# The order in which the sync engine issues the streamed expert tables of a PEER layer

## The reference, cut to what matters

```python
def peer_experts(xn, idx, gates, expert_u, expert_v):
    ...
        u = expert_u[iblk]          # (128 tokens, 128 experts, 1024)
        v = expert_v[iblk]
        act = jax.nn.gelu(jnp.einsum('tkd,td->tk', u, xblk), approximate=False)
        return jnp.einsum('tk,tkd->td', (gblk * act), v)
```

## Time and profile before

| | |
|---|---|
| median of 3 runs | 2571.09 us (2567.44 to 2571.16) |
| profiled execution, its own time | 2571.09 us |
| profiled execution, span from first to last instruction | 2569.4 us |
| TensorE busy | 2479.7 us (97%) |
| VectorE busy | 1968.9 us (77%) |
| GpSimd busy | 1460.1 us (57%) |
| moved by DMA | 857.68 MB, mean 334 GB/s |

### The profile page before, as it was taken

The page is one execution under the profiler, slowest core; times in us unless marked ns, Lnnn a source line. Parts: engine busy times, 40 slices in busy tenths (PEclk is TensorE's granted clock), DMA queues, the critical chain, the costliest instruction groups (busy, mean ns, idle before and its releaser), DMA issues.

```text
span 2569.4 us, 24120 instructions
## 1 busy us (share of the span) xinstructions
PE 2479.7 (97%) x7561; PEld 1364.8 (53%) x7561; DVE 1968.9 (77%) x4252; ACT 425.2 (17%) x783; POOL 1460.1 (57%) x1169
## 2 busy tenths in 40 slices
PE   8999999999788899999999999999999999999998
PEld 7687786867666344444444444444444444444443
DVE  4308889778699888777878877779787777878777
ACT  0213313222787000010011000000000000000001
POOL 0000477678611267666666777667676776766664
PEclk9999999999999999999999999999999999999999
DMA  8544886965778989989999999999999999999997
GB/s 326 219 158 163 321 287 170 364 169 132 211 228 240 351 332 381 377 300 400 405 383 370 383 390 400 387 420 414 420 375 396 405 391 420 398 417 384 420 393 256
DMA packets 288063, 857.68 MB, mean 334 GB/s; under 512 B 42048, under 2 KB 99392, under 8 KB 273344
## 3 DMA queue, kind: packets, MB, share of 16 engines
q0 software_dynamic: 167184, 541.73, 55.7%
q1 hardware_dynamic: 108400, 289.25, 30.0%
q10 hardware_dynamic: 12352, 25.17, 2.6%
HBM read 807.75 MB, written 48.30 MB: 333 GB/s over the span
## 4 chain that ended last, share of the span: by engine, by line
PE 80%; POOL 6%; DVE 5%; DMA 4%; ACT 3%; issue 2%; DVEq 1%; ACTq 0%; SPq 0%
PE pairs L827 34%; PE pairs L781 33%; PE pairs L695 9%; POOL gate_tables L646 5%; PE pairs L713 1%; PE pairs L738 1%; ACT arena L981 1%; DMA arena<-in_w_all 1%; DMA arena<-gate_tables 1%; PE pairs L794 1%; POOL ring L675 1%; DMA ring<-in_expert_u,idx 1%; ACT arena L1005 1%; DMA gate_tables<-gate,place 1%; DVE arena L1463 1%
## 5 line engine op out<-in xcount | busy, mean ns | idle before, releaser
L675 POOL DMA_INDIRECT ring<-in_expert_u,idx x512 | 660.2, 1289 | 606.4 <-DVE dots L1182 342.7
L827 PE MATMUL pairs<-arena 128*128 128x512 f32 x2048 | 884.8, 594 | 8.2 <-DVE arena L1248 8.2
L781 PE MATMUL pairs<-arena 128*128 128x512 f32 x2048 | 882.5, 592 | 0.0
L675 POOL DMA_INDIRECT ring<-in_expert_v,idx x512 | 583.5, 1140 | 298.8 <-DVE arena L1193 133.0
L1182 DVE CUSTOM_DVE_ANT_0 junk<-ring,xf 128x1024 bf16<-128x1024 f32 x512 | 609.7, 1223 | 155.0 <-DMA ring<-in_expert_u,idx 151.6
L827 PEld LDWEIGHTS pairs<-arena 128*128 128x128 f32 x2048 | 390.0, 191 | 500.6 <-issue 499.8
L781 PEld LDWEIGHTS pairs<-arena 128*128 128x128 f32 x2048 | 388.6, 190 | 486.5 <-issue 486.5
L1193 DVE SCALAR_TENSOR_TENSOR arena<-ring,arena 128x1024 f32<-128x1024 f32 x381 | 470.2, 1282 | 55.5 <-DMA ring<-in_expert_v,idx 54.6
L695 PE MATMUL pairs<-arena 128*128 128x256 f32 (+1 forms) x1792 | 399.8, 386 | 7.6 <-ACT arena L942 4.1
L695 PEld LDWEIGHTS pairs<-arena 128*128 128x128 f32 x1792 | 345.6, 193 | 60.0 <-ACT arena L942 5.0
L989 ACT ACTIVATE arena<-pairs 128x512 f32<-128x512 f32 x128 | 76.5, 597 | 1220.2 <-PE pairs L781 1213.9
(11 more groups left out here) (174 smaller groups left out, 1086.2 us busy)
## 6 DMA issues: line engine op xcount, KB each, us to landing
arena<-in_w_all SPq DMA_DIRECT2D x80, 1024.0 KB, 6.0
arena<-in_uT SPq DMA_DIRECT2D x128, 512.0 KB, 6.9
arena<-in_expert_v SPq DMA_DIRECT2D x128, 512.0 KB, 8.8
arena<-gate_tables SPq DMA_DIRECT2D x32, 1024.0 KB, 11.8
gate_tables<-arena SPq DMA_DIRECT2D x11, 2048.0 KB, 9.9
gate_tables<-junk ACTq DMA_DIRECT2D x4, 2048.0 KB, 15.0
ring<-in_expert_u,idx POOLq DMA_INDIRECT x512, 8.9
ring<-in_expert_v,idx POOLq DMA_INDIRECT x512, 8.1
```

The lines of the kernel that those rows point to most:

```text
L675: nc.gpsimd.indirect_dma_start(out=ring[:, r % RING, :], out_offset=None, in_=expert_u if table == "u" else expert_v, in_offset=bass.Indir ...
L781: last = nc.tensor.matmul(score_bank[x], uslot[:, x % USLOTS, k * P:(k + 1) * P], xfT[:, k, :], start=(k == 0), stop=(k == KD - 1))
L827: last = nc.tensor.matmul(o_bank[n % 4], gated[:, x % GSLOTS, t * P:(t + 1) * P], vrows[:, j, half * 512:(half + 1) * 512], start=(j == 0) ...
```

## The change

The sync engine issues the same loads in another order.

- The u tiles 10 to 13 are issued right after the four loads of the sums, before the gate halves 2 and 3, instead of one by one during group 0's pieces.
- After that a u tile is issued as soon as its slot is free: `load_u(a + 4)` at the place of tile a. The four u tiles that begin a tile phase are thus issued at the end of the tile phase before, where they were issued after pieces 1, 2, 4 and 5.
- Each v tile from the third on is issued one tile earlier: three at the end of a group's pieces instead of two, then one beside each of the next five tiles.
- A gate half h is issued at tile 4(h - 1). For even h that is the same place as before. For odd h it is the seventh tile of a tile phase, where it was after the second piece of the following pieces phase.

TensorE, VectorE, ScalarE and GpSimd keep their programs.

```diff
-            assert next_u == EARLY
-            load_gates(2)
-            for g in range(GROUPS):
-                tiles = list(range(VJ * (g + 1) + 2, min(VJ * (g + 2) + 2, KEYS)))
-                for x, sums_done in zip(tiles, (1, 2, 4, 5)):
-                    sp.wait_ge(o_full, SUMS * g + sums_done)
-                    load_u(x)
-                    if sums_done == 2:
-                        load_gates(2 * g + 3)
-                if g + 1 < GROUPS:
-                    load_v(g + 1, 0)
-                    load_v(g + 1, 1)
-                for i, x in enumerate(tiles[:USLOTS + 1]):
-                    if x + USLOTS in tiles:
-                        load_u(x + USLOTS)
-                    sp.wait_ge(s_full, x + 1)
-                    load_v(g + 1, 2 + i)
-                    if i == USLOTS:
-                        load_v(g + 1, 3 + i)
-                    if i == 2 and 2 * g + 4 < HALF_GROUPS:
-                        load_gates(2 * g + 4)
+            while next_u < EARLY + USLOTS:
+                load_u(next_u)
+                next_u += 1
+            pending = []
+            for kind, a, b in dense:
+                if kind == "tile":
+                    if EARLY <= a < KEYS - USLOTS:
+                        load_u(a + USLOTS)
+                    if pending:
+                        load_v(*pending.pop(0))
+                    if a % GJ == 0 and 0 < a and a // GJ + 1 < HALF_GROUPS:
+                        load_gates(a // GJ + 1)
+                elif b == SUMS - 1 and a + 1 < GROUPS:
+                    for j in range(3):
+                        load_v(a + 1, j)
+                    pending = [(a + 1, j) for j in range(3, VJ)]
```

## The result

The changed kernel takes 2582.65 us (median of 5; 2580.3 to 2588.5), the kernel before 2567.44 in the same series (median of 5; 2563.93 to 2571.16). The ratio is 1.0058, 95% interval 1.0041 to 1.0077: 0.58% or 15 us slower. The profiled execution took 2591.22 us, more than any of the five, so its waits are probably somewhat larger than the median's.

What follows compares the result with a forecast made beforehand. Full DMA engines were taken to hold the row stream in tile phases, GpSimd's issuing in pieces phases, TensorE running without waits from 869 us. Group 2 3, u stretches 2, clock 3: 8 us on 2571.1, 2579; 8-in-10 range 2567 to 2597.

Steps and rivals of the forecast that it cites:

- Nothing to win in the last 1690 us, only to lose: From 869 us TensorE runs without waits; load order can't shorten this, only lengthen it through late tiles, gates or sums.
- Loads of their own cost nothing: u and v tiles already land well before use, so their own landing costs nothing and earlier issue gains nothing.
- Bytes moved into the DMA-bound tile phase make rows late: Tile phases go from 14 units to 19, or 17 with a late gate half; rows fall from 28.7–29.9 to about 26.
- Pieces phases return only what GpSimd can issue: Pieces phases win back rows above 31.5: 35 in u stretches (6 us), 38 to 39 in v stretches (12 us).
- Group 2 is the tight place, 3 us: Around group 2's sixth gate and second sum: gate 19.7 us late against 18.3, stall 1.4; 3 us taken, bounds 0 and 6.6.
- The sum's stall of 2.8 us: At group 2's second sum: 22.6 us late against 19.8 of slack, so TensorE stalls 2.8 us.
- The u stretches, 2 us: Groups 5, 6, 9, 10: lateness reaches 16.6 us, 21 at the bound; stall nothing or about 1 us at two places.
- The clock, 3 us: After a TensorE stall the granted clock may drop, costing 0 or 3.2 us at one or two places; one taken.
- The start costs nothing: Group 0: u tiles delay the third gate half, 2.4 us of VectorE, covered by TensorE's banks; nothing taken.
- loss piles up: Rival: with 23.7 rows per tile phase, four u-stretch groups lose 9.2 us each; about 25 us, 2596; chance 0.12.
- the 40 that the prediction named as a sign of being wrong: Pieces phases issuing over 40 rows would show the prediction wrong; it expected the same 34 to 39.
- The other sign, tile phases that keep 29 rows: Tile phases still issuing 29 rows would show the prediction wrong; it expected 24 to 27.

Runs made afterwards that it cites:

- e1: Kernel before, with only the four u tiles that begin a tile phase issued in the tile phase before; ratio to before 1.0006.
- e2: Kernel before, with only the odd gate halves moved to the seventh tile of a tile phase; ratio to before 1.0004.
- e3: Kernel before, with only the third to seventh v tile of a group issued one tile earlier; ratio to before 1.0013.
- e9: Kernel before, with u tiles moved into the tile phase and v tiles one tile earlier, odd gate halves and start as before; ratio to before 1.0002.
- e11: Changed kernel's order from group 0 on, but with the start of the kernel before; ratio to before 1.0035.
- e4: Changed kernel, same issue order, but four u tiles in eight load 128 of 1024 columns (output wrong); ratio to before 1.0005.
- e6: Kernel before, plus three extra 0.524 MB HBM copies in each tile phase of groups 0 to 13; ratio to before 1.0033.
- e7: Changed kernel, plus three extra 0.524 MB HBM copies in each pieces phase of groups 1 to 14; ratio to before 1.0065.
- e10: Kernel before, with u tiles and odd gate halves moved into the tile phase, v tiles and start as before; ratio to before 1.0034.
- e5: Kernel before, with only the start changed: u tiles 10 to 13 right after the sums' loads, then gate halves 2 and 3; ratio 1.0007.
- e12: Kernel before, with each v tile from the second on issued one tile later, spread over the tile phase; ratio to before 1.0032.

## Why the prediction came out, step by step

**Nothing to win in the last 1690 us, only to lose**: right; TensorE had no wait there that an order could take away, and every wait added is in the time.

**Loads of their own cost nothing**: right. In none of the changed kernel, e1, e2, e3 and e9 to e11 does TensorE wait for a streamed tile.

**Bytes moved into the DMA-bound tile phase make rows late**: right, and shown by e4 (bytes out, loss gone) and e6 (bytes in, loss there). 17 units and 25.7 rows are what the prediction worked out for a late gate half. But it isn't enough for a wait: e1 and e9 have 17 units in that phase too, and TensorE doesn't wait. The Trainium skill ("DMA: Bandwidth & Descriptors", Where 436 GB/s comes from) puts loads from HBM at about 358 GB/s a core. The changed kernel's tile phase at 408 and its windows at 419 to 425 don't agree with that, as those of before didn't.

**Pieces phases return only what GpSimd can issue**: right, shown by e7. But the rate was over-sized: 35 rows for u stretches, where the changed kernel issued 32, 33, 33 and 32 in 54.93 us of groups 6, 7, 10 and 11. The 35 came true in e9, whose odd gate half stays 14 us into the phase. That an early gate half makes GpSimd's issues longer would fit (1.44 us each in group 6 against 1.26 in e9), but no run shows how.

**Group 2 is the tight place, 3 us**: the gate part was right. The sixth gate was 20.1 us late for the 19.7 predicted, and TensorE waited 1.65 us for it at 1209.6, for 1.4. The sum's stall of 2.8 us behind it, from which the 3 us were taken, didn't come; 0.96 us for a sum came a tile phase earlier, at 1119.3, where nothing was foreseen. That the two make 2.6 us is in part luck.

**The u stretches, 2 us**: this is the term that was mis-sized. It measured 1.64 + 3.33 us after groups 6 and 7 and 1.13 + 4.04 after groups 10 and 11, 10.1 us. The step took 16.6 us as the peak of lateness; it was 20 to 22. Two things in it were wrong. The net loss of a group was too small: the tile phases of groups 5, 6, 9 and 10, each with 54.93 us of the pieces phase behind it, issued 57, 61, 59 and 61 rows, 14 short of the 63 each that TensorE's pace wants, where the prediction had 61 each, 8 short. And a single tile phase was put on top of the 7 us of before, as if the v stretches recovered all. They didn't: the sixth gate was 8.4 and 13.8 us late in groups 4 and 8, where it was 1.6 in both before, and from there it went 14.2, 20.1, 21.8 in groups 5 to 7 and 17.4, 19.6, 22.5 in groups 9 to 11. The late gate half, counted as a relief for the tile phase, seems to be none for VectorE: with the u tiles moved, e10, which has it, waits, and e9, which hasn't, doesn't.

**The clock, 3 us**: right in size, but by luck: it was taken as one fall of 3.2 us at group 2's stall, and it came as two of some 1.7 us behind the waits of 3.33 and 4.04 us, which the prediction didn't have. Behind the wait of 1.65 us the granted clock stayed at 1.00.

**The start costs nothing**: nearly; VectorE waited for the third gate half as foreseen, but 4.68 us, not 2.4, and TensorE waited 0.19 us in the changed kernel, 1.4 in e5.

**The predicted total** was 8 us; it was 15 in the timed runs. The "loss piles up" rival had the right mechanism for the surplus. Its 25 us were too much because it took 23.7 rows for a tile phase, and groups 5, 6, 9 and 10 issued 25, 28, 26 and 29. The v stretches won back no more than foreseen: groups 8 and 12 issued 41 rows, which passes the 40 that the prediction named as a sign of being wrong, but TensorE's waits had stretched these phases to 60.1 and 60.8 us, and in 54.93 us it was 37 and 36. The other sign, tile phases that keep 29 rows, can be read either way: five of groups 1 to 13 issued 29, but by the bytes moved no tile phase held more than 27.6 rows, where before it was 26.8 to 29.9.

**What stays open.** One pair of parts that brings waits is shown (u tiles and odd gate halves, e10); the v tiles with the gate halves weren't tried. Why the changed kernel (0.58%) loses more than e11 (0.35%) isn't shown: the start is the only difference, it leaves no more lateness in group 1 than e11 has, and the intervals overlap. How late gates are differs between profiles by some 5 us where nothing in the programs says so (e1 and e9 in group 7: 14.3 and 9.0), so single latenesses are to be read as that coarse. That the gate halves count because their bytes come just when VectorE is latest is argued from e9 and e10, not tested by itself.

## What to carry to other kernels

Where a stream of bulk loads and a stream of small gathered reads share full DMA engines, when a bulk load is issued is a choice of which reads it makes late. Put bulk loads where the reads' own issuer is the limit, and fill evenly where the DMA engines are, even if slots stand free earlier (here e12's evenly spread v tiles made the gates less late, though no time was left to win by it). Lateness behind a deep buffer is invisible until it passes the buffer's slack, so parts of a change that each cost nothing can cost 15 us together: measure how late each hand-over is, not only whether anybody waits.

## What the runs showed of the hardware that was not expected

An indirect load of 128 rows of 4 KB on GpSimd took 0.93 to 1.99 us to issue in the changed kernel from 850 us on, but for one of 3.05. GpSimd's rate differs between phases in which next to nothing else holds it: 32 issues in 54.9 us with 45.35 us busy (changed kernel, group 6) and 36 with 43.91 (e9, group 7; its row counts 38, with those that the window's ends cut), with DMA shares of 0.93 and 1.00. Nothing here shows what makes the long ones long.

Three copies of 0.524 MB within HBM raised a pieces phase from 340 to 376 GB/s and cost it no rows (e7, group 6), while the DMA engines' busy share rose only from 0.93 to 0.97: here a share near 1 didn't mean that they carried all they could.
